# Four places for weight and factor tiles, earlier dot products, and factor loads of eight tiles in the last stages of a transformer layer

## The reference, cut to what matters

```python
x = post_norm(x, mx[:, 2] * y_x, ln_g[l, 0], ln_b[l, 0])
hx = modulate(layer_norm(x), mx[:, 3], mx[:, 4])
x = post_norm(x, mx[:, 5] * peer(hx, ...), ln_g[l, 1], ln_b[l, 1])
# peer, for a block of tokens h:
q = (h @ w_query).reshape(t, PEER_HEADS, 2, PEER_KEY_DIM // 2)
top_s, top_i = lax.top_k(scores, PEER_TOPK)          # twice, then the best 16 of 16 x 16
act = gelu(einsum('td,thkd->thk', h, expert_u[expert_idx]))
return einsum('thk,thkd->td', gate * act, expert_v[expert_idx])
```

## Time and profile before

| | us |
|---|---|
| three runs | 2815.94, 2824.56, 2830.46 (median 2824.56) |
| profiled execution | 2836.64 |
| span of its trace | 2834.8 |
| candidate stage | 1446 to 1690 |
| token stage | 1690 to 2045 |
| tail | 2045 to 2145 |
| V stage | 2145 to 2808 |

### The profile page before, as it was taken

How to read it: one execution, slowest core, us unless ns; L and a number is a source line. 1 busy time by engine, 2 the same in 40 slices (tenths; PEclk the granted TensorE clock), 3 DMA queues, 4 the chain that set the end, 5 groups by cost and what they waited for, 6 DMA issues and landing times.

```text
span 2834.8 us, 37454 instructions
## 1 busy us (share of the span) xinstructions
PE 2409.3 (85%) x12641; PEld 2054.1 (72%) x12641; DVE 1639.6 (58%) x3319; ACT 817.0 (29%) x1175; POOL 1220.8 (43%) x681
## 2 busy tenths in 40 slices
PE   6898898898898999949998788888878888888885
PEld 2687686786776767739998788888876666666664
DVE  3565566466466311155585468888655665666657
ACT  3312213213213132223333233434223222323231
POOL 0302302202112124414455545555575666666663
PEclk9998998998998999979999889999999899999998
DMA  5200101101101122313345547888898777777773
GB/s 211 75 31 30 59 15 44 59 15 44 37 32 50 60 76 95 104 52 106 113 140 165 179 128 286 293 306 303 316 370 292 253 275 286 259 285 277 279 287 134
DMA packets 158630, 455.02 MB, mean 161 GB/s; under 512 B 14704, under 2 KB 72176, under 8 KB 157424
## 3 DMA queue, kind: packets, MB, share of 16 engines
q1 hardware_dynamic: 119456, 287.59, 30.2%
q0 software_dynamic: 36864, 134.23, 12.4%
q10 hardware_dynamic: 2256, 32.51, 2.8%
HBM read 401.85 MB, written 52.43 MB: 160 GB/s over the span
## 4 chain that ended last, share of the span: by engine, by line
PE 45%; DMA 18%; POOL 16%; DVE 10%; issue 5%; ACT 5%; SPq 1%; DVEq 1%; ACTq 0%; POOLq 0%
POOL w_lo L874 12%; DMA raw<-w 10%; PE bank L498 8%; PE bank L500 7%; PE bank L499 7%; DMA rows<-peer_u,e_row 4%; DMA gu_dram<-gu 4%; POOL rows L944 4%; DVE cv L1075 3%; PE pair L1623 2%; PE bank L1638 2%; PE bank L1868 2%; PE bank L1631 2%; ACT w_hi L733 2%; DVE dY L1113 1%
## 5 line engine op out<-in xcount | busy, mean ns | idle before, releaser
L874 POOL TENSOR_TENSOR w_lo<-raw,w_hi 128x1024 fp32r<-128x1024 f32 x344 | 844.3, 2456 | 1284.3 <-ACT w_hi L733 613.9
L498 PE MATMUL bank<-lat_hi,w_hi 128*128 128x384 f32 (+1 forms) x1536 | 566.0, 368 | 56.1 <-ACT gu L794 36.0
L500 PE MATMUL bank<-lat_hi,w_lo 128*128 128x384 f32 (+1 forms) x1536 | 548.9, 357 | 0.0
L499 PE MATMUL bank<-lat_lo,w_hi 128*128 128x384 f32 (+1 forms) x1536 | 548.7, 357 | 0.0
L498 PEld LDWEIGHTS bank<-lat_hi,w_hi 128*128 128x128 f32 x1536 | 294.6, 192 | 82.3 <-issue 42.1
L1887 PE MATMUL bank<-w_hi,c_hi 128*128 128x512 f32 x768 | 257.8, 419 | 93.7 <-DVE c_lo L1434 92.3
L733 ACT CAST w_hi<-raw 128x1024 fp32r<-128x1024 f32 x260 | 271.9, 1046 | 192.9 <-DMA raw<-w 192.1
L500 PEld LDWEIGHTS bank<-lat_hi,w_lo 128*128 128x128 f32 x1536 | 293.0, 191 | 21.6
L499 PEld LDWEIGHTS bank<-lat_lo,w_hi 128*128 128x128 f32 x1536 | 294.6, 192 | 17.6
L1887 PEld LDWEIGHTS bank<-w_hi,c_hi 128*128 128x128 f32 x768 | 152.1, 202 | 139.8 <-DVE c_lo L1434 98.2
L1887 PE MATMUL bank<-w_lo,c_hi 128*128 128x512 f32 x768 | 252.0, 411 | 0.0
(11 more groups left out here) (340 smaller groups left out, 3757.5 us busy)
## 6 DMA issues: line engine op xcount, KB each, us to landing
raw<-w SPq DMA_DIRECT2D x344, 512.0 KB, 3.7
gu_dram<-gu SPq DMA_DIRECT2D x128, 192.0 KB, 4.6
g_dram<-gs ACTq DMA_DIRECT2D x6, 4096.0 KB, 17.6
gl<-gu_dram SPq DMA_DIRECT2D x32, 768.0 KB, 7.6
gq<-g_dram SPq DMA_DIRECT2D x32, 768.0 KB, 10.8
ada<-w_ada SPq DMA_DIRECT2D x32, 512.0 KB, 3.8
ada_a<-w_ada SPq DMA_DIRECT2D x8, 512.0 KB, 9.1
xin<-x SPq DMA_DIRECT2D x4, 512.0 KB, 12.5
```

What stands on the lines that cost most here:

```text
L498: nc.tensor.matmul(out, hi, rh, start=start, stop=False)
L499: nc.tensor.matmul(out, hi, rl, start=False, stop=False)
L500: return nc.tensor.matmul(out, lo, rh, start=False, stop=stop)
L874: nc.gpsimd.tensor_sub(w_lo[:, slot, :], raw[:, slot % RAW, :], w_hi[:, slot, :].bitcast(F32)).then_inc(split_done, 1)
```

## The change

- `RAW` becomes 4 from `T_QUERY` on: tile n is requested when tile n - 4 is split (`next_late`). Two places are the old ones, two (`raw_more`) lie where `x1` was. So `x1` (the residual) is stored to `x1_dram` before the query stage, the first two loads into the new places wait for that store and for the norm, ACT splits two query tiles after the norm instead of before it, and at the end `x1` is read back into the four raw places.
- `gu` has four places; SP stores the gelu of a tile ahead of the next split it waits for.
- The Exp of the candidate stage is issued behind the ninth tile of a block.
- 33 dots move into the candidate stage (11 in each of blocks 1 to 3, in four portions), the token stage has six dots for four tiles (72), the tail 19, and the last four run beside the first V tiles. `tile_of` moves the gathers with them.
- `gl` and `gq` have two slots of eight tiles. ACT requests them: slot 0 behind V tile 9 of a round of 16 (and the first one in the tail, at tile 118), slot 1 behind tile 1. The pieces of `gq` are 2048 bytes long instead of 1024.
- Some semaphores of the first half are merged; nothing else is moved there.

```diff
-N_IT = PK // 8 - 1
+V_LOAD = 8
+N_IT = PK // (2 * V_LOAD) - 1
-DOT_G = 8 * (DT // 32)
+DOT_CD = 11
+DOT_T = 6
+DOT_G = (LAT - 1) * DOT_CD
+DOT_END = DOT_G + DOT_T * (DT // 32)
-RAW = 2
+RAW = 4
+        raw_more = after.branch()("raw_more", [2, KB * P])
-        gu = after("gu", [2, DT])
+        gu = after("gu", [4, DT])
-        gq = after("gq", [2, DT // GTOK, 4, GTOK])
-        gl = after("gl", [2, 4, DT])
+        gl = [m("gl%d" % j, [V_LOAD, DT]) for j, m in enumerate((after, spare))]
+        gq = [m("gq%d" % j, [DT // GTOK, V_LOAD, GTOK]) for j, m in enumerate((after, spare))]
+            def next_late(i, n):
+
+                sp_.wait_ge(split_done, i + (n + 1))
+                load_w(i + (n + RAW), n % RAW)
+            sp_.wait_ge(ln_bias, LAT)
+            sp_.dma_start(x1_dram.rearrange("b p n -> p b n"), x1[:, :, :]).then_inc(x1_out, 16)
+            sp_.wait_ge(ln_out, NCH + 2 * LAT)
+            sp_.wait_ge(x1_out, 16)
+            for j in range(2, RAW):
+                load_w(T_QUERY + j, j)
                 for j in range(4):
-                    next_w(i * 4, T_U + j)
                     store_gu(i * 4 + (2 * PH - 4), j)
+                    next_late(i * 4, T_U + j)
+            for m in range(2):
+                hi_n(T_QUERY + 2 + m)
             act.wait_ge(hin_lo, 2 * KB + KB)
             act.dma_start(sk[:, :, :], A["sub_keys"]).then_inc(ld_late, 16)
-                act.wait_ge(cd, b * CD_N + CD_EXP)
-                nc.scalar.activation(bf[5][:, :, :], bf[4][:, :, :], ACT.Exp).then_inc(cd_exp, 1)
+                    if j == 8:
+                        act.wait_ge(cd, b * CD_N + CD_EXP)
+                        nc.scalar.activation(bf[5][:, :, :], bf[4][:, :, :], ACT.Exp).then_inc(cd_exp, 1)
+            def act_v(i, y0, y1, last):
+
+                for y in range(y0, y1):
+                    act.wait_ge(v_mm, i * 16 + (y + 1))
+                    act_c(i * 16, y + 4)
+                    hi_n(T_V + RING + y, i, 16)
+                    if y == 0:
+                        act.wait_ge(cf_done, i * 16)
+                        load_gl(i * 2 + 1, 1)
+                        load_gq(i * 2 + 1, 1)
+                    if y == V_LOAD and not last:
+                        act.wait_ge(cf_done, i * 16 + V_LOAD)
+                        load_gl(i * 2 + 2, 0)
+                        load_gq(i * 2 + 2, 0)
+                u = T_U - 2 * PH + RING + 2
                 if q < ROWS:
-                    return T_U - 2 * PH + X_CD + 2 * U_CD + RING
+                    return u + X_CD + U_CD - 1
-                    return T_U - 2 * PH + X_G + n // 2 + RING + 1
+                    return u + X_CD + U_CD + 2 + n * U_CD // DOT_CD
+                if n < DOT_END:
+                    return u + X_G + (n - DOT_G) * 4 // DOT_T
                 if n < P:
-                    return T_U - 2 * PH + X_END + RING + 1 + (n - DOT_G) // 3
+                    return u + X_END + (n - DOT_END) * (PK - X_END) // (P - DOT_END)
+                def block_dots(part):
+                    if b:
+                        for m in range(part * DOT_CD // 4, (part + 1) * DOT_CD // 4):
+                            dot(0, (b - 1) * DOT_CD + m)
```

More of the change, by code:

```diff
@@ L466, in units, with raw_at @@
             return t[:, :, :].rearrange("p (g d c) n -> p g d c n", g=NG, d=NDIR)
+        def raw_at(slot):
+            return raw[:, slot, :] if slot < 2 else raw_more[:, slot - 2, :]
         def unit(d, chunk):
@@ L511, in load_w @@
             def load_w(n, slot):
-                sp_.dma_start(raw[:, slot, :], A["w"][n]).then_inc(raw_full[slot], 16)
+                sp_.dma_start(raw_at(slot), A["w"][n]).then_inc(raw_full[slot], 16)
             def load_ada(m, slot):
@@ L608, in _, with v_loads @@
-            v_loads(0, 4, True, False)
+                next_late(0, T_V + j)
+            def v_loads(r_, first, last):
+                for y in range(4 if first else 0, 2 * V_LOAD):
+                    if not last or y < 2 * V_LOAD - RAW:
+                        next_late(r_ * (2 * V_LOAD), T_V + y)
+                    else:
+                        b = y - (2 * V_LOAD - RAW)
+                        sp_.wait_ge(split_done, T_ALL - RAW + b + 1)
+                        sp_.dma_start(raw_at(b), x1_dram[b]).then_inc(raw_full[b], 16)
@@ L792, in act_u @@
                 act.wait_ge(a_mm, i * per + (x + 1))
-                act.wait_ge(gu_st[x % 2], i * (per * 8) + x // 2 * 16)
-                nc.scalar.activation(gu[:, x % 2, :], bank[6 + x % 2][:, 0:DT], ACT.Gelu).then_inc(gelu, 1)
+                act.wait_ge(gu_st[x % 4], i * (per * 4) + x // 4 * 16)
+                nc.scalar.activation(gu[:, x % 4, :], bank[6 + x % 2][:, 0:DT], ACT.Gelu).then_inc(gelu, 1)
             with act.Fori(0, 2 * PH // 4) as i:
@@ L1340, in candidates @@
                 synced()
+                block_dots(0)
                 base = made[0]
@@ L1419, in _, with token_block @@
-            for q in range(DOT_G, P):
+            def token_block(i, first):
+                for g in range(32):
+                    if g >= 2 or not first:
+                        dve.wait_ge(g_mm, i * 32 + (g - 1))
+                    marks(i, g)
+                    for m in range(DOT_T * g // 8, DOT_T * (g + 1) // 8):
+                        dot(i, DOT_G + m)
+            token_block(0, True)
+            with dve.Fori(1, DT // P) as i:
+                token_block(i, False)
+            for q in range(DOT_END, P - 4):
@@ L1446, in add_row @@
                 else:
-                    nc.vector.scalar_tensor_tensor(pair[:, :], rows[:, x, :], weight, pair[:, :], ALU.mult,
+                    nc.vector.scalar_tensor_tensor(pair[:, :], rows[:, x % ROWS, :], weight, pair[:, :], ALU.mult,
                                                    ALU.add).then_inc(row_used, 1)
```

267 lines of the change are left out of this document (128 added, 139 removed).

## The result

| | before | after | |
|---|---|---|---|
| median, us | 2827.51 (4 runs) | 2741.44 (2728.58 to 2747.08, 4 runs) | ratio 0.9695, 95% interval 0.9649 to 0.9742 |
| span of the profiled execution | 2834.8 | 2726.8 | -108.0 |

What follows compares the result with a forecast made beforehand. In the V stage no engine was taken as the bound but the order of loads in SP's one queue. Terms +1 - 20 - 43 - 20 - 74 = -156 took the median 2824.6 to 2669 us, range 2600 to 2735.

Steps and rivals of the forecast that it cites:

- V stage: Main V tiles: 4.6 us a tile, 589 us from 663, so -74; bounds 531 us (-132) and 640 (-23).
- slow restart: V tiles: PE resuming slowly after a stall, named beside 4.6 us a tile.
- rival A: V stage: factor loads fully hidden, 4.2 to 4.3 us a tile, -118 instead of -74, 2625 us; chance 0.17.
- The queue decides who waits behind whom: V stage: moving factor loads to ACT's queue helps since weight loads no longer stand behind them; ACT's 192 us go away.
- Token stage: 48 tiles: fewer dots, four raw and gelu places, 4 us lost per 4 MB store; 310 to 312 us from 355, -43.
- Candidate stage: U tiles: PE no longer waits for gelu, block 1 loses 5 us, blocks 2 and 3 take 51 to 53 each; -20.
- Tail: Last 16 tiles before the V tiles: fewer gathers, 4.4 us a tile at 375 GB/s; 80 us from 100, -20.
- Start and end: Start of the query stage +1, bounds 0 and +5; reading x1 back at the end 0 to +2.
- B: Rival, V stage: the eight-tile load is the new bound, landing after 30 us; 4.95 a tile, -29, 2714 us; chance 0.16.
- D: Rival, V stage: the load on ACT's queue starves, landing 35 us from request; slower, 2841 us at 36; chance 0.05.
- C: Rival: DVE becomes the bound, candidate blocks 60 us each (+8), token stage gains only 15; 2725 us; chance 0.07.
- E: Rival: DMA engines, not order, were the limit; V stage unchanged, the rest half, -41, 2784 us; chance 0.05.

Runs made afterwards that it cites:

- early loads: Changed kernel with each factor load of the V stage requested five tiles sooner, when its slot is read out: 2678.3 us, ratio 0.948 to the kernel before.
- both edits: Changed kernel with factor loads requested five tiles sooner and ACT casting w_hi ahead of c_hi: 2649.4 us, ratio 0.939 to the kernel before.
- weight cast first: Changed kernel with ACT casting w_hi ahead of c_hi: 2765.4 us, ratio 0.979; with factor loads also in SP's queue 2674.2 us, 0.944.
- experiment 1: Changed kernel against versions with w_hi cast ahead of c_hi, factor loads five tiles sooner, or both: ratios to the kernel before 0.979, 0.948 and 0.939.

## Why the prediction was wrong

**V stage, the term that failed.** The step is "The 3 to 5 us left are a stall of PE in each eight tiles, about 0.45 us a tile. So 4.6 with a slow restart": the slow restart is named and nothing is added for it. Forecast were 128 x 4.15 = 531 us of work and 58 of stall, 589. Found were 527 of work, 57 of waits and 38 by which matmuls took longer at a lower granted clock, 33 of these right behind a wait: 622. The restart is as large as the 33 us that were missed. The rows had it: the V stage of before shows a clock of 0.92 for 663 us.

**The stall came out right by luck.** The prediction gave the load 21.3 us from its request, "when PE ends the ninth tile of a round", and a stall of 3 to 5 us means a landing in 24 to 26. It had 17.2 us and landed in 20.5. The request goes out some 5 us late because ACT's casts ahead of it wait for the ring, and the landing was that much shorter. "So no engine is the bound" left the ring out: I added up each engine's busy time, did not follow a tile through all four, and did not ask what the product costs beside a split. With early loads the ring is PE's pace (4.43), so rival A's 4.2 to 4.3 is not reached by this change; both edits reach it (4.20). The trace of before had hints: `c_lo` at 1496 ns beside `cf` at 610, two instructions of the same size, and the stage's longest wait, which the earlier trace rows leave out:

```profile
ACT c_hi L846 <- DVE cf L1428: 252.8, 107, 8.5
```

**The queue.** "The queue decides who waits behind whom" was right, and the conclusion the wrong way round. I counted it as a gain that weights no longer stand behind the load. They can stand, having four places; the load can't. On ACT's queue it shares each DMA engine with two others and lands 5 us later (23.1 against 17.6). In the prediction I weighed the Trainium skill ("DMA: Bandwidth & Descriptors", Issuing engines are not separate DMA queues), by which the move would bring nothing. With the weight cast first in both, ACT's queue cost 96 us of V stage (655 against 559). It costs that only to a load that is asked for late: with early loads on ACT's queue `gq` landed in 24.8 us and the stage took 538. Early loads on SP's queue were not tried.

**Token stage.** The mechanism held: rows beside the 4 MB stores, some 4 us lost to each (26.4 us of waits, 24 forecast). The size did not: 324 where 286 + 26 make 312, the rest being PE at a lower granted clock after each pause (299 us busy instead of 284). It is the error of the V stage again: I had taken PE's 5.95 a tile as fixed.

**Candidate stage.** Block 1 ended at 1563.2 (forecast 1564) with a PE wait of 20.6 us (forecast 15); blocks 2 and 3 took 53.4 and 54.8 (forecast 51 to 53). -14 instead of -20.

**Tail.** -27 instead of -20: the DMA engines were full as forecast (1.03), but moved 413 GB/s, not the 375 of the earlier trace rows.

**Start and end.** 0 for the start as a term (TensorE began the query stage 6.6 us behind the last input before, 6.7 after); the 3.4 us in which the profiled execution was ahead come from the first half.

**The range.** The stages above miss the forecast by 48 us together (-108 against -156), and the medians by 70; the other 22 are the choice of executions. Every stage from the candidate stage on lies within its own bounds, yet the sum lies outside 2600 to 2735. The candidate, token and V terms all missed to the same side, and they are not independent: all three rest on loads that arrive just in time and on a PE that restarts at full clock. "The ends taken not all at once" gave too little for that.

**The rivals.** B asked for a landing over 30 us, D for 35; neither came. C forecast blocks of 60 us, not found. E's unchanged V stage isn't there either. Its doubt, that the DMA share would stay near 0.75, came true (0.79), though by PE's waits and not by a limit of the engines: they reach 0.91 in experiment 1 with both edits.

## What to carry to other kernels

Put a price on each pause of TensorE and on the slow stretch behind it: in the V stage 57 us of waits brought 38 more, in the token stage 21 brought 16. Where engines hand a tile round in a ring, walk the ring in the timeline and add up its steps with their durations as they are beside each other; then ask both whether it is slower than TensorE and which request stands behind one of its steps. Check a sum such as "8 x the ring's pace + the wait" against TensorE's own row: here 8 x 4.39 + 3.8 gives the right total, 38.9 us a round, though TensorE goes at 4.12 and then at half clock. Of two loads in competition, let the one with a deadline go first in one queue and the one with spare places wait behind it, and ask for it when its slot falls free, not when it is needed. A lead of one tile in an issue table may be worth more than a doubled buffer: check such constants against the longest landing.

## What the hardware did that I had not expected

- A DVE instruction with two inputs in SBUF and 384 columns takes 0.55 us alone and up to 2.77 when it begins within POOL's subtraction; in the kernel after, each `cf` that begins 0.06 to 0.20 us into a split ends 0.41 to 0.42 us behind it, so it gets hardly anything done meanwhile. POOL's own instruction stays at 2.38 to 2.43 us in the rows of the V stage. `pair`, with one input in PSUM, is never stretched (1278 ns, at most 1290; of those in the kernel before 24 begin within a split and take 1287 at most). Where DVE begins first it is POOL that is stretched, to 4.30 us in the candidate stage of the kernel after, beside the first of two `hot` (2.29 us):

```profile
1587.48 6.71 DVE L1425 TENSOR_TENSOR hot<-bf,cst 128x2048 f32<-128x2048 f32 x2
1587.73 4.30 POOL L921 TENSOR_TENSOR w_lo<-raw,w_hi 128x1024 fp32r<-128x1024 f32 x1 [1.73 <-ACT w_hi L746]
```

  The Trainium skill ("SBUF — State Buffer", Who interferes with whom) says that a DVE instruction with two SBUF inputs contends with a GpSimd one that reads SBUF, and that the order of issue decides who blocks; its Summary: rules for kernel authors has the second of such a pair fully blocked until the first finishes. The trace agrees, with the numbers above.
- DVE, ACT and POOL have two rhythms beside each other, 4.39 us a tile with `cf` stretched and 3.70 with `c_lo` stretched; a weight cast that came 0.78 us late turned one into the other for the rest of the stage.
- Later requests went with a shorter stage: with the weight tiles asked for two splits later the 1.5 MB of `gq` landed 2.7 us sooner. That run does not part this from the ring, which held for fewer tiles.
- After a wait of 3 to 5 us in the V stage TensorE's next tile took 5.8 to 7.1 us instead of 4.12, at a mean granted clock of 0.71 to 0.57, with stretches at 0.50, the 1.2 GHz level, in it; the token stage shows the same behind waits of 2 to 3 us.
